# Convolved feed-forward: one 512-wide matmul for high weights, VectorE adds the halves, GpSimd takes the scaling, the product and the low parts

## The chip, the cores and the metric

The kernel runs on one core of a Trainium2 chip. The metric is the device time of one execution in microseconds (us), the median over several runs. A core has five engines that run their own instruction streams and meet at semaphores: PE (TensorE, matmuls), DVE (VectorE), ACT (ScalarE), POOL (GpSimd) and SP (here only the issuer of the weight stream's transfers). In the profile PEld is PE's weight load.

## The reference, cut to what matters

The program is a whole first transformer block with four mixers, followed by a second block of two layers. The change touches one stage of the first block, its feed-forward network with a short causal convolution over the sequence. With `x` the normed rows (256 tokens, 1024 wide):

```python
u = x @ w_up                         # 1024 -> 2 * 2816: gate half and value half
u = conv_w[2]*u[t] + conv_w[1]*u[t-1] + conv_w[0]*u[t-2] + conv_b
hidden = silu(gate) * value          # 2816 wide
out = hidden @ w_down                # 2816 -> 1024, then normed and added to h
```

All of it is float32. Matmuls are done in split form: every operand is a high part (rounded to the matmul's float32r) and a low part (what the rounding left), and a product is high*high + high*low + low*high, three matmuls that add into one PSUM sum.

## The kernel before

**The weight stream.** All weights come from one DRAM tensor in slots of 1 MB (128 partitions x 2048 columns). SP loads slot n into a ring of four once slot n-4 is used up. ACT copies a loaded slot to its high part (`split_high`, L436, output `high`), and DVE subtracts to get the low part (`split_low`, L447, `low<-raw,high`), which lies over the raw slot. PE may start on a slot when its low part is there. ACT and DVE keep three slots ahead of the one just used: in step f of the stage below they split the slot of tile f+3.

**The convolved stage (`Ffn` with `conv=True`).** Its up phase runs over 22 tiles f of 128 hidden features. A tile uses one slot: 8 pieces for the gate and 8 for the value (`part` 0 and 1). The weight piece is the stationary operand, and the 256 tokens of `xh` or `xl` are the moving one: `mm3` (L481 to L483) gives three matmuls of 256 columns for each piece, 48 for a tile, into one PSUM bank `f % 4`. From there each tile goes through a chain of small steps, with its buffers in the tile `square`:

- DVE L1335 multiplies the sums by the row of inverse norms (`inv_row`) into `scaled_in`, 512 wide;
- ACT L1299 (twice, 256 wide) applies tap 2 and the bias into `mixed`;
- DVE L1353 (four times) adds taps 1 and 0, both operands in SBUF;
- ACT L1307 applies Silu to the gate;
- DVE L1365 multiplies gate and value into `product`;
- ACT L1311 copies the product's high part into `hh`, and DVE L1369 subtracts the low part into `hl`.

DVE and ACT run a hand-written order: in step f DVE does the scaling of tile f, the taps of tile f-1, product and low part of earlier tiles, then one `split_low`. Engines work their queues strictly in order, so a wait in a row holds all rows behind it.

**The down phase** (`Residual.tensor`) then runs over 22 tiles of `hh` and `hl`, 11 slots in all, with 512-wide matmuls into banks 4 to 7. It takes the next stage's slots from the same ring, and 24 dummy matmuls (L494) stand at its end. GpSimd in this stage only starts transfers (`Loads`): two that spread bias rows in DRAM, then one of bias into SBUF (L580). All engines meet at the end of a stage (L2720), GpSimd with its transfers landed.

Of the kernel before, what the change touches and what calls it, by code (L numbers as in the profile page):

```python
# [31 lines left out]
P = 128  # L32
S = 256
# [265 lines left out]
def pack_band_bias(x):  # L299
# [15 lines left out]
         "keys_scored", "keys_positive", "keys_summed", "lam_sums", "lam_exps", "masks_added"]  # L315
# [14 lines left out]
class Core:  # L330


    def __init__(self, nc, stream):
# [14 lines left out]
        self.xh = t("xh", [P, KT, S], F32R)  # L348
        self.xl = t("xl", [P, KT, S], F32R)
# [717 lines left out]
class Residual(Stage):  # L1067
# [69 lines left out]
    def row_factor(self, b):  # L1137
        return self.factor
# [100 lines left out]
class Ffn(Residual):  # L1239
# [16 lines left out]

    def row_factor(self, b):
        return self.core.inv[:, 4 + b:5 + b]

    def tensor(self, pe, s):  # L1260
        c = self.core
        self.rows.begin(pe, s)
        for f in range(FT):
            if f == 1:
                self.rows.row(pe, s)
            if f >= 4:
                pe.wait_ge(s["partial_ready" if self.conv else "gates_ready"], f - 3)
            for part in range(2):
                for k in range(KT):
                    if f == 0 and part == 0:  # L1270
# [3 lines left out]
                    last = mm3(pe, c.bank[f % 4][:, part * S:(part + 1) * S], c.piece(pe, self.up, i),  # L1274
                               (c.xh[:, k, :], c.xl[:, k, :]), k == 0, k == KT - 1)
                    c.release(last, self.up, i)
        super().tensor(pe, s)
# [4 lines left out]
    def scalar(self, act, s):  # L1282
# [4 lines left out]
        late = 1 if self.conv else 0  # L1287

        c.split_high(act, self.up.first)
        for step in range(FT + 1 + late):  # L1290
            if step < FT:
                c.split_high(act, self.up.first + step + 1)
            if step < FT and self.conv:
                f = step
# [8 lines left out]
            if 0 <= step - late < FT:  # L1303
                f = step - late
                act.wait_ge(s["convolved"], f + 1)
                gate = self.mixed[:, f % 3, 0:S] if self.conv else self.silu[:, f % 3, :]
                act.activation(gate, gate, ACT.Silu).then_inc(s["inputs_ready"], 1)  # L1307
            if 0 <= step - late - 1 < FT:
                f = step - late - 1
# [4 lines left out]
    def vector(self, dve, s):  # L1314
# [5 lines left out]
        taps, late = 0, 1 if self.conv else 0  # L1320
        row = c.inv_row[:, :]

        c.split_low(dve, self.up.first)
        for step in range(FT + 2 + late):
            if step < FT:
                f = step
# [3 lines left out]
                ps = c.bank[f % 4]  # L1330
                if self.conv:
                    if f >= 2:
                        dve.wait_ge(s["scores_ready"], f - 1)
                        dve.wait_ge(s["convolved"], f - 1)
# [1451 lines left out]
```

## Time and profile before

| what | us |
|---|---|
| median of 3 runs | 1660.08 |
| lowest and highest of them | 1658.35, 1664.02 |
| the profiled execution's own time | 1660.82 |
| its span, first to last instruction | 1659.0 |
| convolved stage, up phase: first matmul to first one of the down phase | 299.16 to 428.22 |
| its down phase, to the dummy matmuls | 428.22 to 488.09 |

Times in rows are us from the span's start. A matmul's own duration in a row is its latency; how fast matmuls follow each other is read from their starts or from their count in a window. A row with xN merges N instructions. Text in brackets at the end of a row is idle time of that engine before it, and what ended it.

### The profile page before, as it was taken

To read this page: it belongs to the slowest core of one execution; us is meant where nothing else is said; L and a number is where in the kernel's file an instruction comes from. 1 tells how busy PE (TensorE), PEld (TensorE's weight loads), DVE (VectorE), ACT (ScalarE), POOL (GpSimd) and SP (SyncE) were. 2 spreads that over 40 slices of the span, in tenths; PEclk is the share of its full clock that TensorE was granted. 3 is DMA by queue.
4 is the path that set the end of the run, shared out by engine and by line. 5 is a ranking of instruction groups with operands and counts; after the bars stand their busy time and mean duration, and the time that the engine had idled before them with its cause. 6 is when DMAs were issued, how large, how long until landed. Compare 5 with 4: busy or idle time off the path is not lost.

```text
span 1659.0 us, 21003 instructions
## 1 busy us (share of the span) xinstructions
PE 1612.4 (97%) x8524; PEld 1364.0 (82%) x8524; DVE 1018.5 (61%) x1379; ACT 863.3 (52%) x1193; POOL 33.7 (2%) x35
## 2 busy tenths in 40 slices
PE   9989999999999999999899999999999999999998
PEld 8878877999888888877777888888888888778887
DVE  5565578698755554568866555455544775765543
ACT  5365675566545443555666444354434565654441
POOL 0000002000000000002000000000000000000000
PEclk9999999999999999999999999999999999999999
DMA  7742324765544555544243655555554533435543
GB/s 286 289 167 108 127 104 176 286 225 189 183 178 178 180 185 193 178 152 153 71 159 130 222 181 180 201 177 178 188 192 178 178 127 127 152 128 190 191 178 127
DMA packets 42959, 289.95 MB, mean 175 GB/s; under 512 B 5048, under 2 KB 5198, under 8 KB 9968
## 3 DMA queue, kind: packets, MB, share of 16 engines
q1 hardware_dynamic: 38272, 271.93, 45.5%
q0 software_dynamic: 4592, 16.69, 2.9%
q8 instruction: 68, 1.11, 0.3%
q14 instruction: 27, 0.22, 0.0%
HBM read 287.51 MB, written 8.55 MB: 178 GB/s over the span
## 4 chain that ended last, share of the span: by engine, by line
PE 87%; DVE 6%; ACT 3%; DMA 2%; issue 1%; DVEq 0%; PEldq 0%; SPq 0%; ACTq 0%; POOL 0%; PEld 0%
PE bank L481 26%; PE bank L483 26%; PE bank L482 25%; PE bank L487 5%; DVE low L447 2%; DMA raw<-stream_dram 2%; PE bank L763 1%; ACT high L436 1%; PE bank L1401 1%; PE bank L645 1%; DMA h<-x_dram 0%; PE bank L1989 0%; PE bank L1843 0%; DVE h L1182 0%; DVE prob L1796 0%
## 5 line engine op out<-in xcount | busy, mean ns | idle before, releaser
L447 DVE TENSOR_TENSOR low<-raw,high 128x2048 fp32r<-128x2048 f32 x254 | 581.2, 2297 | 376.6 <-ACT high L436 376.0
L436 ACT ACTIVATE high<-raw 128x2048 fp32r<-128x2048 f32 x256 | 486.9, 1913 | 350.3 <-DMA raw<-stream_dram 345.6
L481 PE MATMUL bank<-high,xh 128*128 128x512 f32 (+1 forms) x1232 | 486.1, 395 | 6.5 <-DVEq L2720 3.5
L483 PE MATMUL bank<-high,xl 128*128 128x512 f32 (+1 forms) x1232 | 477.8, 388 | 0.0
L482 PE MATMUL bank<-low,xh 128*128 128x512 f32 (+1 forms) x1232 | 477.1, 387 | 0.0
L481 PEld LDWEIGHTS bank<-high,xh 128*128 128x128 f32 x1232 | 232.1, 188 | 54.7 <-DVE low L447 4.6
L483 PEld LDWEIGHTS bank<-high,xl 128*128 128x128 f32 x1232 | 231.9, 188 | 48.4
L482 PEld LDWEIGHTS bank<-low,xh 128*128 128x128 f32 x1232 | 232.3, 189 | 44.5
L481 PE MATMUL bank<-high,hh 128*128 128x512 f32 x440 | 171.9, 391 | 0.0
L483 PE MATMUL bank<-high,hl 128*128 128x512 f32 x440 | 171.3, 389 | 0.0
L482 PE MATMUL bank<-low,hh 128*128 128x512 f32 x440 | 171.2, 389 | 0.0
L481 PE MATMUL bank<-xh,high 128*128 128x256 f32 x472 | 134.3, 285 | 1.2 <-DVE low L447 1.2
L482 PE MATMUL bank<-xl,high 128*128 128x256 f32 x472 | 133.6, 283 | 0.0
L483 PE MATMUL bank<-xh,low 128*128 128x256 f32 x472 | 133.5, 283 | 0.0
L1452 ACT ACTIVATE square<-bank,inv 128x256 f32<-128x256 f32 x88 | 41.7, 475 | 150.0 <-PE bank L483 150.0
L483 PEld LDWEIGHTS bank<-high,hl 128*128 128x128 f32 x440 | 82.6, 188 | 17.3
L482 PEld LDWEIGHTS bank<-low,hh 128*128 128x128 f32 x440 | 82.6, 188 | 16.9
L481 PEld LDWEIGHTS bank<-high,hh 128*128 128x128 f32 x440 | 82.6, 188 | 16.9
L481 PEld LDWEIGHTS bank<-xh,high 128*128 128x128 f32 x472 | 90.6, 192 | 2.2 <-issue 2.2
L482 PEld LDWEIGHTS bank<-xl,high 128*128 128x128 f32 x472 | 90.6, 192 | 0.0
L483 PEld LDWEIGHTS bank<-xh,low 128*128 128x128 f32 x472 | 90.6, 192 | 0.0
L1475 DVE TENSOR_TENSOR square<-square,bank 128x256 f32<-128x256 f32 x88 | 37.1, 422 | 72.7 <-ACT square L1452 72.7
(242 smaller groups left out, 1522.2 us busy)
## 6 DMA issues: line engine op xcount, KB each, us to landing
raw<-stream_dram SPq DMA_DIRECT2D x257, 1024.0 KB, 4.8
band_wide_dram<-band_rows_dram POOLq DMA_DIRECT2D x1, 3072.0 KB, 33.4
t_wide_dram<-t_rows_dram POOLq DMA_DIRECT2D x1, 2304.0 KB, 17.1
u<-mem_dram POOLq DMA_DIRECT2D x2, 1024.0 KB, 5.1
bias<-band_wide_dram POOLq DMA_DIRECT2D x1, 2048.0 KB, 14.3
rel_wide_dram<-rel_rows_dram POOLq DMA_DIRECT2D x1, 1920.0 KB, 17.1
bias<-t_wide_dram POOLq DMA_DIRECT2D x1, 1536.0 KB, 10.7
bias<-rel_wide_dram POOLq DMA_DIRECT2D x1, 1280.0 KB, 7.0
```

The source lines that it names most:

```text
L436: act.activation(self.high[:, n % RING, :], self.raw[:, n % RING, :], ACT.Copy).then_inc(self.high_split, 1)
L447: dve.tensor_tensor(self.low[:, n % RING, :], self.raw[:, n % RING, :], self.high[:, n % RING, :].bitcast(F32), ALU.subtract).then_inc(sel ...
L481: pe.matmul(out, lh, rh, start=start, stop=False)
L482: pe.matmul(out, lh, rl, start=False, stop=False)
L483: return pe.matmul(out, ll, rh, start=False, stop=stop)
L487: return pe.matmul(out, left, right, start=start, stop=stop)
L645: last = pe.transpose(self.bank(g)[0:width, j * P:(j + 1) * P], src, self.core.ident)
L763: last = pe.transpose(self.bank(k)[:, at:at + P], self.rows[:, b, from_tile:from_tile + P], self.core.ident)
L1401: last = pe.transpose(self.turned(c)[:, at:at + P], self.product_rows[:, c % 2, b, j * P:(j + 1) * P], self.core.ident)
L1452: act.activation(self.gate_rows[:, c % 2, b, :], self.sums(c, b)[:, 0:S], ACT.Silu, scale=core.inv[:, 2 + b:3 + b]).then_inc(s["inputs_rea ...
L1475: dve.tensor_tensor(self.product_rows[:, c % 2, b, :], self.gate_rows[:, c % 2, b, :], self.sums(c, b)[:, S:HALF], ALU.mult).then_inc(s["g ...
```

## The change

- `xh` and `xl` become the two halves of one tile `xhl`, so that one access reads 256 columns of high rows and 256 of low rows as a 512-wide moving operand.
- `mm_both` takes the place of `mm3` in the up phase: one 512-wide matmul with the high weights (sums of high rows in the bank's left half, of low rows in its right half), and one 256-wide matmul with the low weights into the left half. Each part of a tile now takes a bank of its own, eight in all.
- ACT copies the right halves to SBUF (`c.t`, twice 256 wide), and DVE adds left half and copy into `scaled_in` (twice 256 wide, `halves_added`).
- GpSimd runs a loop of its own: it scales `scaled_in` by the row (512 wide), makes the product and the low part. It starts its transfers behind this loop, where they stood at the stage's start.
- Silu comes one step later, the copy of the high part too. The other two classes of the stage keep their code.

```diff
+def mm_both(pe, out, weights, rows, start, stop):
+    high, low = weights
+    pe.matmul(out, high, rows, start=start, stop=False)
+    return pe.matmul(out[:, 0:S], low, rows[:, 0, :], start=False, stop=stop)
...
+    def gpsimd(self, pool, s):
...
+        for step in range(FT + 4 if self.conv else 0):
+            f = step
+            if f < FT:
+                pool.wait_ge(s["halves_added"], 2 * f + 2)
...
+                pool.tensor_tensor(scaled, scaled, row, ALU.mult).then_inc(s["partial_ready"], 1)
+            f = step - 4
+            if f >= 0:
+                pool.wait_ge(s["highs_ready"], f + 1)
+                pool.tensor_tensor(c.hl[:, f, :], self.product[:, f % 2, :], c.hh[:, f, :].bitcast(F32), ALU.subtract)\
+                    .then_inc(s["hidden_ready"], 1)
+            f = step - 2
+            if 0 <= f < FT:
+                pool.wait_ge(s["inputs_ready"], f + 1)
+                if f >= 2:
+                    pool.wait_ge(s["hidden_ready"], f - 1)
+                pool.tensor_tensor(self.product[:, f % 2, :], self.mixed[:, f % 3, 0:S], self.mixed[:, f % 3, S:HALF],
+                                   ALU.mult).then_inc(s["gates_ready"], 1)
+        Residual.gpsimd(self, pool, s)
...
-                    last = mm3(pe, c.bank[f % 4][:, part * S:(part + 1) * S], c.piece(pe, self.up, i),
-                               (c.xh[:, k, :], c.xl[:, k, :]), k == 0, k == KT - 1)
+                    last = mm_both(pe, self.sums(f, part), c.piece(pe, self.up, i), c.xhl[:, :, k, :],
+                                   k == 0, k == KT - 1)
...
+                act.wait_ge(c.slot_used, self.up.first + f + 1)
...
+                    last = act.activation(c.t[:, 2 * (f % 2) + part, :], self.sums(f, part)[:, S:HALF], ACT.Copy)
+                last.then_inc(s["side_copied"], 1)
+                c.split_high(act, self.up.first + f + 1)
...
+                dve.wait_ge(s["side_copied"], f + 1)
+                for part in range(2):
+                    dve.tensor_tensor(self.scaled_in[:, f % 2, part * S:(part + 1) * S], self.sums(f, part)[:, 0:S],
+                                      c.t[:, 2 * (f % 2) + part, :], ALU.add).then_inc(s["halves_added"], 1)
```

On DVE, in the middle of the up phase, one step before (L1335 scaling, L1353 taps, L1365 product, L1369 low part, L447 weight split):

```order
L1335 TENSOR_TENSOR square<-bank,inv_row 128x512 [waits convolved_even,scores_ready_even,slot_used]
L1353 SCALAR_TENSOR_TENSOR square<-square,param 128x255 [waits scores_ready_even]
L1353 SCALAR_TENSOR_TENSOR square<-square,param 128x255
L1353 SCALAR_TENSOR_TENSOR square<-square,param 128x254 [waits dve_step_even] x2
L1365 TENSOR_TENSOR square<-square 128x256 [waits hidden_ready_even,inputs_ready_even]
L1369 TENSOR_TENSOR hl<-square,hh 128x256 [waits highs_ready_even]
L447 TENSOR_TENSOR low<-raw,high 128x2048 [waits high_split]
```

The same step on DVE after the change (L1375 adds, L1387 taps):

```order
L1375 TENSOR_TENSOR square<-bank,t 128x256 [waits convolved_even,side_copied_even,scores_ready_even,slot_used]
L1375 TENSOR_TENSOR square<-bank,t 128x256
L1387 SCALAR_TENSOR_TENSOR square<-square,param 128x255 [waits scores_ready_even]
L1387 SCALAR_TENSOR_TENSOR square<-square,param 128x255
L1387 SCALAR_TENSOR_TENSOR square<-square,param 128x254 [waits dve_step_even] x2
L447 TENSOR_TENSOR low<-raw,high 128x2048 [waits high_split]
```

Product and low part have left DVE's step, and its first row now waits for ACT's copy as well (`side_copied`).

On POOL after the change, the last full step of the up phase and the end of its loop (L1277 scaling, L1281 low part, L1288 product, L589 transfers); before, the three transfers were all that it had in this stage:

```order
L1277 TENSOR_TENSOR square<-square,inv_row 128x512 [waits halves_added_even]
L1281 TENSOR_TENSOR hl<-square,hh 128x256 [waits highs_ready_even]
L1288 TENSOR_TENSOR square<-square 128x256 [waits hidden_ready_even,inputs_ready_even]
L1281 TENSOR_TENSOR hl<-square,hh 128x256 [waits highs_ready_even]
L1288 TENSOR_TENSOR square<-square 128x256 [waits hidden_ready_even,inputs_ready_even]
L1281 TENSOR_TENSOR hl<-square,hh 128x256 [waits highs_ready_even]
L1288 TENSOR_TENSOR square<-square 128x256 [waits hidden_ready_even,inputs_ready_even]
L1281 TENSOR_TENSOR hl<-square,hh 128x256 [waits highs_ready_even] x2
L589 DMA t_wide_dram<-t_rows_dram 1536x1x384
L589 DMA band_wide_dram<-band_rows_dram 2048x1x384
L589 DMA bias<-t_wide_dram 128x12x256 [waits loaded]
```

The first three rows are one step, of three operations, each with all operands in SBUF; the transfers stand behind the last low part.

On ACT after the change, the last of the 22 steps (L1332 copies, L436 weight split, L1339 Silu, L1346 tap 2 and bias, L1353 high part) and the end of the loop:

```order
L1332 ACTIVATE t<-bank 128x256 [waits halves_added_even,slot_used]
L1332 ACTIVATE t<-bank 128x256
L436 ACTIVATE high<-raw 128x2048 [waits slot_loaded1]
L1339 ACTIVATE square<-square 128x256 [waits convolved_even]
L1346 ACTIVATE square<-square,param 128x256 [waits gates_ready_even,partial_ready_even]
L1346 ACTIVATE square<-square,param 128x256
L1353 ACTIVATE hh<-square 128x256 [waits gates_ready_even]
L1339 ACTIVATE square<-square 128x256 [waits convolved_even]
L1353 ACTIVATE hh<-square 128x256 [waits gates_ready_even]
L1339 ACTIVATE square<-square 128x256 [waits convolved_even]
L1353 ACTIVATE hh<-square 128x256 [waits gates_ready_even] x2
L436 ACTIVATE high<-raw 128x2048 [waits slot_loaded2]
```

The copies stand ahead of the weight split, and the split of the down phase's fourth slot stands behind the last tile's whole chain.

## Rows read from the trace of the kernel before

**Rows 1.** The page: busy us, share of span and instructions of each engine.

```profile
PE 1612.4 (97%) x8524; PEld 1364.0 (82%) x8524; DVE 1018.5 (61%) x1379; ACT 863.3 (52%) x1193; POOL 33.7 (2%) x35
```

**Rows 2.** Busy time by windows: up phase's middle, down phase's middle, granted clock behind.

```profile
core 0: us, PE busy (x) PEld busy (x) DVE busy (x) ACT busy (x) POOL busy (x), PEclk, DMA share, GB/s
...
430.00:485.00 55.00, 55.00 (x244) 45.53 (x244) 29.51 (x29) 23.17 (x23) 0.00 (x0) 1.00 0.54 191
360.00:400.00 40.00, 40.00 (x335) 40.00 (x335) 35.65 (x56) 25.24 (x36) 0.00 (x0) 1.00 0.52 185
```

**Rows 3.** Timeline of PE: start us, us, engine, line, operation, count.

```profile
428.22 0.40 PE L481 MATMUL bank<-high,hh 128*128 128x512 f32 x1
...
488.09 3.03 PE L494 MATMUL bank<-xh 128*128 128x256 f32 x24
```

**Rows 4.** Timeline of DVE: one step of the up phase, to the next's start.

```profile
334.01 0.69 DVE L1335 TENSOR_TENSOR square<-bank,inv_row 128x512 f32<-128x512 f32 x1
334.61 1.66 DVE L1353 SCALAR_TENSOR_TENSOR square<-square,param 128x255 f32<-128x255 f32 x4
336.18 0.42 DVE L1365 TENSOR_TENSOR square<-square 128x256 f32<-128x256 f32 x1
336.52 0.42 DVE L1369 TENSOR_TENSOR hl<-square,hh 128x256 fp32r<-128x256 f32 x1
336.85 2.29 DVE L447 TENSOR_TENSOR low<-raw,high 128x2048 fp32r<-128x2048 f32 x1
339.06 0.69 DVE L1335 TENSOR_TENSOR square<-bank,inv_row 128x512 f32<-128x512 f32 x1
```

**Rows 5.** Timeline of ACT: reads of a bank, then two rows of a step.

```profile
297.92 3.72 ACT L772 ACTIVATE xh<-bank,param 128x256 fp32r<-128x256 f32 x8 [2.50 <-PE bank L763]
...
346.33 1.08 ACT L1299 ACTIVATE square<-square,param 128x256 f32<-128x256 f32 x2
347.31 0.40 ACT L1307 ACTIVATE square<-square 128x256 f32<-128x256 f32 x1
```

**Rows 6.** Timeline of POOL and DVE in the merge stage, where both work.

```profile
249.84 2.56 POOL L1652 TENSOR_TENSOR xn<-xn,u 128x512 f32<-128x512 f32 x2 [189.33 <-DVE u L1621]
249.75 2.05 DVE L1621 TENSOR_TENSOR u<-u,bank 128x512 f32<-128x512 f32 x3
...
252.35 3.34 POOL L1652 TENSOR_TENSOR xn<-xn,u 128x512 f32<-128x512 f32 x1
254.47 3.38 DVE L447 TENSOR_TENSOR low<-raw,high 128x2048 fp32r<-128x2048 f32 x1
255.65 3.34 POOL L1652 TENSOR_TENSOR xn<-xn,u 128x512 f32<-128x512 f32 x1
```

**Rows 7.** POOL and DVE in a later stage; last, DVE L2101 (min/median/max ns).

```profile
779.68 0.72 POOL L1686 TENSOR_TENSOR u<-bias,taken 128x256 f32<-128x256 f32 x1 [96.83 <-ACTq L2720]
788.23 1.27 POOL L1686 TENSOR_TENSOR u<-bias,taken 128x512 f32<-128x512 f32 x1
788.85 0.67 DVE L2101 TENSOR_TENSOR rden<-rden,small 128x2 f32<-128x2 f32 x1
L2101 DVE TENSOR_TENSOR rden<-rden,small x16: 160/161/665, 142.8 to 799.5; 128x2 f32<-128x2 f32 x16
```

**Rows 8.** The stage's transfers, the late slot; PE's waits (total us, times, longest).

```profile
298.32 1.13 POOL L580 DMA_DIRECT2D t_wide_dram<-t_rows_dram  x1 [39.33 <-DVEq L2720]
333.12 1.05 POOL L580 DMA_DIRECT2D bias<-t_wide_dram  x1 [32.60 <-DMA band_wide_dram<-band_rows_dram]
bias<-t_wide_dram POOLq DMA_DIRECT2D x1, 1536.0 KB, 10.7
320.09 1.91 ACT L436 ACTIVATE high<-raw 128x2048 fp32r<-128x2048 f32 x1 [9.62 <-DMA raw<-stream_dram]
PE bank L481 <- DVE low L447: 1.6, 2, 1.2
```

**Rows 9.** Timeline of DVE: the first tile's scaling.

```profile
308.65 0.69 DVE L1335 TENSOR_TENSOR square<-bank,inv_row 128x512 f32<-128x512 f32 x1
```

**Rows 10.** Busy time by windows: attention, where PE has gaps (columns: PE, PEclk, DMA).

```profile
800.00:812.00 12.00, 10.02 (x78) 1.00 0.00 0
```

More of the change, by code:

```diff
@@ L347, in __init__ @@
         self.h = t("h", [P, NB, D])
[L348 to L349 removed]
+        self.xhl = t("xhl", [P, 2, KT, S], F32R)
+        self.xh, self.xl = self.xhl[:, 0, :, :], self.xhl[:, 1, :, :]
         arena = self.top
@@ L1255, in __init__, with sums @@
         self.scaled_in = part(2 * S + 3 * HALF, 2, HALF)
+    def sums(self, f, part):
+        return self.core.bank[2 * (f % 4) + part][:, :]
+    def gpsimd(self, pool, s):
+        c = self.core
+        row = c.inv_row[:, :].unsqueeze(1).to_broadcast([P, 2, S])
+        for step in range(FT + 4 if self.conv else 0):
+            f = step
+            if f < FT:
+                pool.wait_ge(s["halves_added"], 2 * f + 2)
+                scaled = self.scaled_in[:, f % 2, :].rearrange("p (a t) -> p a t", a=2)
+                pool.tensor_tensor(scaled, scaled, row, ALU.mult).then_inc(s["partial_ready"], 1)
[12 more added lines that the diff above has]
+        Residual.gpsimd(self, pool, s)
     def row_factor(self, b):
@@ L1286, in scalar @@
         bias = PARAM(c.param, "conv_b")
-        late = 1 if self.conv else 0
         c.split_high(act, self.up.first)
[L1290 to L1294, printed above, removed]
+        for step in range(FT + 3):
+            f = step
+            if f < FT:
+                act.wait_ge(c.slot_used, self.up.first + f + 1)
+                if f >= 2:
+                    act.wait_ge(s["halves_added"], 2 * f - 2)
+                for part in range(2):
+                    last = act.activation(c.t[:, 2 * (f % 2) + part, :], self.sums(f, part)[:, S:HALF], ACT.Copy)
+                last.then_inc(s["side_copied"], 1)
+                c.split_high(act, self.up.first + f + 1)
+            f = step - 2
+            if 0 <= f < FT:
+                act.wait_ge(s["convolved"], f + 1)
+                gate = self.mixed[:, f % 3, 0:S]
+                act.activation(gate, gate, ACT.Silu).then_inc(s["inputs_ready"], 1)
+            f = step
+            if f < FT:
                 act.wait_ge(s["partial_ready"], f + 1)
@@ L1302, in scalar @@
                 last.then_inc(s["scores_ready"], 1)
[L1303 to L1309, printed above, removed]
+            f = step - 3
+            if 0 <= f < FT:
                 act.wait_ge(s["gates_ready"], f + 1)
@@ L1319, in vector @@
         w = PARAM(c.param, "conv_w").rearrange("p (j f) -> p j f", j=3)
-        taps, late = 0, 1 if self.conv else 0
-        row = c.inv_row[:, :]
         c.split_low(dve, self.up.first)
-        for step in range(FT + 2 + late):
-            if step < FT:
-                f = step
+        for step in range(FT + 1):
+            f = step
+            if f < FT:
                 dve.wait_ge(c.slot_used, self.up.first + f + 1)
```

39 lines of the change are left out of this document (9 added, 30 removed).

## Prediction

> **What bounds the kernel now.** I read the page's first part, then busy time by windows around the changed stage, then the timelines of DVE and ACT inside it, and last every place where POOL computes. On the page PE is busy for 97% of the span and POOL for 2% [rows 1]. In the middle of the up phase PE starts 335 matmuls in 40 us, 119.4 ns each at full granted clock, while DVE is busy for 35.65 of the 40 [rows 2]: PE sets the pace, DVE comes next. A tile costs PE 48 x 119.4 ns = 5.73 us. One step of DVE from one scaling to the next takes 339.06 - 334.01 = 5.05 us [rows 4], with no gap in it, so DVE has 0.68 us to spare per tile. This spare time is all that the stage has on that engine.
>
> **PE's part.** In the down phase 244 matmuls, 512 wide, start in 55 us, 225.4 ns each [rows 2]. So a 512-wide and a 256-wide one cost 344.8 ns where three 256-wide ones cost 358.2 [rows 2]: no column is saved, only 13.4 ns of fixed cost per piece. A tile falls from 5.73 to 16 x 344.8 ns = 5.52 us, and 22 tiles save 22 x 0.21 = 4.7 us, 0.3% of the kernel. The Trainium skill ("TensorE: Matmul & The Clock Gate", Back-to-back issue gap) gives a warm start-to-start time of N/2.4 ns plus about 2.5 ns, by which one start fewer per piece would save some 0.9 us in all, an estimate; the rows here show more per start, and I go by the rows.
>
> **DVE's part, alone.** From the step's starts in [rows 4]: the 512-wide scaling 0.60, the taps 1.57, product 0.34, low part 0.33, weight split 2.21. Scaling, product and low part leave (1.27). Two 256-wide adds come; as one 256-wide row holds the queue 0.34, they cost 0.68. DVE alone would need 5.05 - 1.27 + 0.68 = 4.46 us per tile.
>
> **POOL's part, alone.** Nearest rows: 0.72 us for a 256-wide operation on two SBUF operands, 1.27 for a 512-wide one [rows 7]. A step's three operations take 1.27 + 2 x 0.72 = 2.71. Taken engine by engine all is below PE's 5.52, and the change would win its 4.7. That is the reading that I don't follow, for the next reason.
>
> **What the two do to each other.** In the merge stage POOL's 512-wide operations take 1.28 us beside DVE rows with one operand in a bank, and those DVE rows keep their 0.68 (three in 2.05) [rows 6]. But beside the weight split, whose operands are both in SBUF, each waits for the whole of the other: POOL 3.34, the split 3.38 instead of 2.29, POOL 3.34 [rows 6]. The ends are 255.69 (POOL), 257.85 (DVE) and 258.99 (POOL): 2.16 for the split, 1.14 for the POOL operation, one after the other, 3.30 a pair. A DVE operation of 2 columns with both operands in SBUF takes 0.67 instead of 0.16 and ends with the POOL operation that it met [rows 7]. In the changed stage four taps and the split of every DVE step have both operands in SBUF, and so have all three POOL operations; only the adds (one operand in a bank) are free of it. No row shows a tap (scalar_tensor_tensor) beside POOL; I take it to behave like the split, since what they share is two SBUF operands.
>
> The Trainium skill ("SBUF — State Buffer", Who interferes with whom) says that any DVE instruction with two SBUF inputs contends with a GpSimd instruction that reads SBUF, and that the later one waits for all of the earlier one. The trace agrees where it can show it (3.34 and 3.38 above); for the taps no row does. By that rule the sum below stands; without it for the taps, the first rival does.
>
> **The step after.** A 256-wide POOL operation holds DVE for its 0.72 less the 0.14 that the 512-wide one loses (1.28 to 1.14): 0.58. So DVE's step is adds 0.68 + taps 1.57 + split and POOL's scaling 3.30 + two more holds 1.16 = 6.71 us, longer than PE's 5.52. Why all of POOL's work falls there: the scaling of tile f is released by DVE's own adds, and DVE goes straight on to taps; product and low part follow on POOL at once, as Silu of that tile was done during the step before. ACT stays hidden: copies 0.93 (2 of 3.72/8, [rows 5]), split 1.91 [rows 8], Silu 0.40, taps' first part 0.98 (to the next start), high copy as long as Silu, 0.40 [rows 5], together 4.6. From below the step is 6.71 - 0.68 = 6.03, if POOL gets a full 0.68 beside the adds; from above 4.46 + 2.71 = 7.17, with POOL's whole durations. I take 6.71, from the rows of just this pair.
>
> **The sum.** DVE's first add stands where the first scaling did, 308.65 [rows 9]. Behind the adds (0.68) the weight split starts at once and holds up POOL's scaling: 308.65 + 0.68 + 2.16 = 311.5. Then scaling 1.14, ACT's two rows 0.98, its copies of the next tile 0.93, three hand-overs of 0.1 (my estimate): step 1 begins at 314.8. Step 1 has the scaling alone on POOL, 0.68 + 1.57 + 3.30 = 5.55, to 320.4; steps 2 and 3 a product more, 6.13 each, to 332.6; steps 4 to 21 are full, 18 x 6.71 = 120.8, to 453.4. PE waits from about tile 7 on, some 1.2 us per tile, since each step's split frees a tile three further on. The last three splits are those of the down phase's first three slots, the third at 453.4, and PE works on it until 453.4 + 5.44 = 458.8 (59.87 us for 11 slots, [rows 3]). The fourth slot's high copy stands on ACT behind the last tile's whole chain: taps with two POOL holds 2.73, Silu 0.40, product 0.72, high copy 0.40, ACT's split 1.91, DVE's 2.29, six hand-overs 0.6, together 9.05, to 462.5. Eight slots remain, 43.5 us: the down phase ends at 506.0, where it ended at 488.09 [rows 3]. That is 17.9 us later: 1660.8 + 17.9 = 1678.7 by the profiled execution, and as this lies 0.7 above the median of the runs, **1678**. The part before the stage and the stages behind it keep their code; I cost them at nothing.
>
> **The moved transfers.** Before, they start at 298.32 and hold the weight stream up: ACT waits 9.62 us for one slot and PE at most 1.2 us [rows 8]. That wait goes, but gives nothing, as DVE's chain is then what PE waits for. They now start behind POOL's last low part, at about 459. The two spreads take 333.12 - 298.32 = 34.8 us and the bias 1.05 + 10.7 [rows 8], to about 506; PE ends its dummy matmuls 3 us after 506.0. So they are just covered. Bounds: nothing, or up to 2 us of slot waits on PE (the 1.2 scaled to two late slots) and up to 6 us if they last 10 us longer and the stage's end waits for POOL. I take nothing, the burst meeting a ring that filled while PE waited.
>
> **Rivals.**
> - *The taps don't exclude POOL.* Then only the split waits, for at most product and low part: 4.46 + 1.16 = 5.62 a step. 314.8 + 21 x 5.62 = 432.8, the chain of the last tile without its two holds 7.9, to 440.7, eight slots, 484.2: 3.9 us earlier, **1656** for the median, not slower. For it: no row shows a tap beside POOL. Against it: the three kinds of DVE row that are shown differ in just the operands' place. Chance 0.10.
> - *PE keeps the pace throughout*, since POOL slips in between: -4.7 and the 1.2 of the late slot, **1654**. It needs DVE's step below 5.52, and the holds alone bring it to 6.03 at the least. 0.04.
> - *More is lost:* POOL's full durations (18 x 0.46 = 8.3 more) or transfers that outlast the stage (6 more): **1686 to 1693**. For it: three hand-overs a tile between POOL and others, for which no row has a price. 0.06 beyond the forecast's own range.
> - *The clock falls*, as PE now has a gap in each tile: a tile of 11 us, **1700 and far more**. Against it: PE was busy for 10.02 of 12 us in attention and kept the granted clock of 1.00 [rows 10], and 5.52 of 6.71 is about the same share. 0.02.
>
> **How the numbers follow.** The forecast has 0.78. Its own range goes by the step's bounds: 18 x 0.68 = 12.2 less is 1666, 18 x 0.46 = 8.3 more is 1686. About 0.3%, 5 us, is what a measurement of this kernel can tell from no change. The range from 1661 to 1691 holds the forecast and most of the third rival and leaves out the first two and the fourth. Faster by over 0.3%: 0.04 (the second rival). Within: 0.12 (the first, and 0.02 of the forecast's lower end). Slower: 0.84.
>
> **What would show it.** In the profile after: DVE's four taps with POOL between them, about 3.9 us from the first tap to the split where it was 1.57; starts of the adds 6.7 us apart; PE waiting for `low` about 1.2 us at nearly each tile from the seventh on and some 3.6 us ahead of the down phase's fourth slot; matmuls of a tile at 5.5 us when they run. The forecast is wrong if the taps keep 0.39 us each beside POOL rows, or if POOL's rows fall mainly beside the adds.

## Result, and the profile after

The changed kernel takes 1681.03 us (median of 4 runs, 1679.15 to 1683.04), the kernel before, run beside it, 1662.05 us (4 runs, 1658.35 to 1664.21). The ratio is 1.0112 with an interval of 1.0092 to 1.0132: slower by 19.0 us, where the prediction said 1678, 17.9 us more than before. The profiled execution took 1680.24 us, its span is 1678.4 us, 19.4 us longer than before at the same granted clock (0.995 and 0.996).

The page's first line now, to be read beside [rows 1]:

```profile
PE 1615.1 (96%) x8172; PEld 1346.4 (80%) x8172; DVE 1045.0 (62%) x1357; ACT 872.4 (52%) x1237; POOL 105.3 (6%) x101
```

PE starts 352 matmuls fewer. DVE has 22 instructions fewer and 26.5 us more busy time. That is the whole case in one row: work was taken off DVE, and DVE became longer. The timeline of DVE shows one step in the middle of the up phase, to the next step's adds (compare [rows 4]):

```profile
383.50 0.74 DVE L1375 TENSOR_TENSOR square<-bank,t 128x256 f32<-128x256 f32 x2
384.17 3.68 DVE L1387 SCALAR_TENSOR_TENSOR square<-square,param 128x255 f32<-128x255 f32 x4
387.77 2.28 DVE L447 TENSOR_TENSOR low<-raw,high 128x2048 fp32r<-128x2048 f32 x1
389.98 0.74 DVE L1375 TENSOR_TENSOR square<-bank,t 128x256 f32<-128x256 f32 x2
```

From start to start the adds take 0.67 us, the four taps 3.60 (1.57 before), the split 2.21; the step is 6.48 us here and 6.49 as the mean of the 18 full steps (331.80 to 448.65).

The timeline of POOL in the same step has its three rows beside the taps:

```profile
384.32 1.48 POOL L1277 TENSOR_TENSOR square<-square,inv_row 128x512 f32<-128x512 f32 x1 [3.23 <-DVE square L1375]
385.76 0.92 POOL L1281 TENSOR_TENSOR hl<-square,hh 128x256 fp32r<-128x256 f32 x1
386.82 0.75 POOL L1288 TENSOR_TENSOR square<-square 128x256 f32<-128x256 f32 x1
```

The first steps, in which POOL's rows arrive one by one, give the price of each. In this timeline of DVE, step 1 has only POOL's scaling, step 2 the product as well:

```profile
315.03 2.70 DVE L1387 SCALAR_TENSOR_TENSOR square<-square,param 128x255 f32<-128x255 f32 x4
317.65 2.28 DVE L447 TENSOR_TENSOR low<-raw,high 128x2048 fp32r<-128x2048 f32 x1
...
320.51 3.19 DVE L1387 SCALAR_TENSOR_TENSOR square<-square,param 128x255 f32<-128x255 f32 x4
323.62 2.28 DVE L447 TENSOR_TENSOR low<-raw,high 128x2048 fp32r<-128x2048 f32 x1
```

The taps take 2.62 us, then 3.11, then 3.60 in the full steps, after 1.57 before: POOL's 512-wide row holds DVE (DVE stands still for it) for 1.05 us, each 256-wide one for 0.49. These are the rows' own durations, 1.28 and 0.72 [rows 6, 7], less 0.23 each time.

PE's waits for `low` in the up phase (us in all, times, longest), where before there were two of 1.6 us together [rows 8]:

```profile
PE bank L495 <- DVE low L447: 8.3, 14, 0.7
```

Five more, 7.9 us in all, stand in the down phase, and one of 3.08 ahead of the next stage. The timeline of PE has the fourth down slot, a later slot, the dummy matmuls and the next stage's start (`DVEq L2741` is DVE's arrival at the meeting that ends the stage):

```profile
457.27 0.47 PE L481 MATMUL bank<-high,hh 128*128 128x512 f32 x1 [2.70 <-DVE low L447]
...
481.71 0.47 PE L481 MATMUL bank<-high,hh 128*128 128x512 f32 x1 [2.43 <-DVE low L447]
...
503.59 3.03 PE L503 MATMUL bank<-xhl 128*128 128x256 f32 x24
...
509.70 1.07 PE L772 MATMUL bank<-const,h 128*128 128x128 f32 x8 [3.08 <-DVEq L2741]
```

The wait at 457.27 is the last tile's chain. The waits at 481.71 and 509.70 come from weight slots that land late, as two rows of ACT show:

```profile
477.32 1.92 ACT L436 ACTIVATE high<-raw 128x2048 fp32r<-128x2048 f32 x1 [15.08 <-DMA raw<-stream_dram]
...
502.31 1.92 ACT L436 ACTIVATE high<-raw 128x2048 fp32r<-128x2048 f32 x1 [2.67 <-DMA raw<-stream_dram]
```

The moved transfers run from 453.87 to about 502.4 us, and a weight slot takes longer to land while they do. Time from issue to landing of the slots issued from 457 to 505 us, after the change and, for comparison, in the run below that spreads the transfers out:

```profile
DMA to landing us min/median/max: 4.8/9.8/14.3
```

```profile
DMA to landing us min/median/max: 4.7/4.8/4.9
```

The 14.3 belong to the slot that ACT splits at 477.32; it was issued at 463.0.

The down phase ends 15.50 us later than before (503.59 against 488.09), the next stage begins 18.05 later (509.70 against 491.65), and within that stage another 1.36 us go, between two groups of its transposes (511.19 to 514.22, before 493.14 to 494.81). PE does not wait there; its granted clock is at the lower of its two levels, 1.2 GHz instead of 2.4. Busy time by windows of that place after the change, and of the same place before (PE busy, matmuls begun, granted clock, DMA share, GB/s):

```profile
511.00:514.00 3.00, 2.81 (x8) 0.50 0.00 0
```

```profile
493.00:496.00 3.00, 2.86 (x15) 1.00 0.38 158
```

From there to the end the two traces keep their distance of 19.4.

### The profile page after: what moved, and what is told of

The parts are those of the page before. It is cut to its first block, busy times and chain, and to the rows that moved or that the text cites. A ratio compares the mean times of both kernels' runs of the same rounds, so it can differ in the third digit from the quotient of the medians.

```text
span 1678.4 us, 20429 instructions
## 1 busy us (share of the span) xinstructions
PE 1615.1 (96%) x8172; PEld 1346.4 (80%) x8172; DVE 1045.0 (62%) x1357; ACT 872.4 (52%) x1237; POOL 105.3 (6%) x101
## 4 chain that ended last, share of the span: by engine, by line
PE 78%; DVE 11%; issue 4%; ACT 3%; DMA 3%; POOL 1%; DVEq 0%; SPq 0%; ACTq 0%; PEldq 0%; PEld 0%
PE bank L481 23%; PE bank L483 23%; PE bank L482 23%; PE bank L487 5%; DVE square L1387 4%; DVE low L447 2%; DMA raw<-stream_dram 2%; PE bank L772 2%; ACT high L436 1%; PE bank L1422 1%; DVE square L1375 1%; PE bank L654 1%; POOL square L1277 0%; DMA h<-x_dram 0%; PE bank L2010 0%
## 5 line engine op out<-in xcount | busy, mean ns | idle before, releaser
L447 DVE TENSOR_TENSOR low<-raw,high 128x2048 fp32r<-128x2048 f32 x254 | 580.9, 2296 | 373.8 <-ACT high L436 373.2
L436 ACT ACTIVATE high<-raw 128x2048 fp32r<-128x2048 f32 x256 | 486.6, 1913 | 320.7 <-DMA raw<-stream_dram 314.1
L481 PE MATMUL bank<-high,xhl 128*128 128x512 f32 (+1 forms) x1232 | 487.2, 395 | 6.9 <-DVEq L2741 4.8
L483 PE MATMUL bank<-high,xhl 128*128 128x512 f32 (+1 forms) x1232 | 478.8, 389 | 0.0
L482 PE MATMUL bank<-low,xhl 128*128 128x512 f32 (+1 forms) x1232 | 477.9, 388 | 0.0
L481 PEld LDWEIGHTS bank<-high,xhl 128*128 128x128 f32 x1232 | 233.0, 189 | 55.0 <-DVE low L447 6.0
L483 PEld LDWEIGHTS bank<-high,xhl 128*128 128x128 f32 x1232 | 232.4, 189 | 48.5
L482 PEld LDWEIGHTS bank<-low,xhl 128*128 128x128 f32 x1232 | 233.1, 189 | 44.6
L495 PE MATMUL bank<-xhl,high 128*128 128x512 f32 x352 | 125.4, 399 | 8.3 <-DVE low L447 8.3
L481 PEld LDWEIGHTS bank<-high,hh 128*128 128x128 f32 x440 | 82.6, 188 | 26.5 <-issue 9.7
L496 PE MATMUL bank<-xhl,low 128*128 128x256 f32 x352 | 98.5, 280 | 0.0
L495 PEld LDWEIGHTS bank<-xhl,high 128*128 128x128 f32 x352 | 66.0, 187 | 26.9 <-issue 12.3
L1387 DVE SCALAR_TENSOR_TENSOR square<-square,param 128x255 f32<-128x255 f32 (+1 forms) x88 | 77.7, 941 | 0.0
L781 ACT ACTIVATE xhl<-bank,param 128x256 fp32r<-128x256 f32 x96 | 38.1, 478 | 55.3 <-PE bank L772 55.0
L496 PEld LDWEIGHTS bank<-xhl,low 128*128 128x128 f32 x352 | 66.4, 189 | 0.0
```

Source lines behind the costliest of these rows:

```text
L436: act.activation(self.high[:, n % RING, :], self.raw[:, n % RING, :], ACT.Copy).then_inc(self.high_split, 1)
L447: dve.tensor_tensor(self.low[:, n % RING, :], self.raw[:, n % RING, :], self.high[:, n % RING, :].bitcast(F32), ALU.subtract).then_inc(sel ...
L481: pe.matmul(out, lh, rh, start=start, stop=False)
L482: pe.matmul(out, lh, rl, start=False, stop=False)
L483: return pe.matmul(out, ll, rh, start=False, stop=stop)
L495: pe.matmul(out, high, rows, start=start, stop=False)
```

## Experiments

Two theories stood against each other. **Holds:** two operands in SBUF are what DVE and POOL cannot have at once, so POOL's rows lengthen DVE's step. **Hand-overs:** the chain through POOL, with its semaphores, sets the step, whatever the operands. Beside them the moved transfers were open: the prediction took them at nothing. "Stage" below is the time from PE's first transposes of the convolved stage to those of the next: 194.17 us before, 212.38 after. "Up phase" is counted from the same transposes to the down phase's first matmul, some 1.7 us more than in the table of the time before: 130.74 us before, 138.10 after.

### All vector work back on DVE

```diff
...
-        for step in range(FT + 4 if self.conv else 0):
...
+                dve.wait_ge(s["halves_added"], 2 * f + 2)
...
+                dve.tensor_tensor(scaled, scaled, row, ALU.mult).then_inc(s["partial_ready"], 1)
...
+                dve.tensor_tensor(c.hl[:, f, :], self.product[:, f % 2, :], c.hh[:, f, :].bitcast(F32), ALU.subtract)\
...
+                dve.tensor_tensor(self.product[:, f % 2, :], self.mixed[:, f % 3, 0:S], self.mixed[:, f % 3, S:HALF],
+                                  ALU.mult).then_inc(s["gates_ready"], 1)
```

> The changed kernel with the two-matmul form kept, but scaling, product and low part back on DVE; GpSimd only starts its transfers, at the stage's start as in the kernel before. Exclusion theory (DVE and POOL wait for each other when both read two operands in SBUF): no POOL work, so no holds. DVE's step is adds 0.66 + scaling about 0.57 + taps 1.57 + product 0.34 + low part 0.33 + weight split 2.20 = 5.67 us, the taps at 0.39 each; the stage is back within 3 us of before, 1658 to 1665 us, although DVE has 1.2 us more work per tile than in the changed kernel. Rival (the two-matmul form, the ACT copies or the longer chain of hand-overs cost the time, not POOL): the step stays near 6.4 us and the time at 1675 us or above.

Measured: 1671.35 us (8 runs, 1667.41 to 1674.08), ratio 1.0042 (1.0026 to 1.0058). Timeline of DVE:

```profile
384.29 0.75 DVE L1357 TENSOR_TENSOR square<-bank,t 128x256 f32<-128x256 f32 x2
385.07 0.69 DVE L1361 TENSOR_TENSOR square<-square,inv_row 128x512 f32<-128x512 f32 x1
385.69 1.66 DVE L1372 SCALAR_TENSOR_TENSOR square<-square,param 128x255 f32<-128x255 f32 x4
387.26 0.42 DVE L1380 TENSOR_TENSOR hl<-square,hh 128x256 fp32r<-128x256 f32 x1
387.78 0.42 DVE L1387 TENSOR_TENSOR square<-square 128x256 f32<-128x256 f32 x1
388.12 2.29 DVE L447 TENSOR_TENSOR low<-raw,high 128x2048 fp32r<-128x2048 f32 x1
390.33 0.75 DVE L1357 TENSOR_TENSOR square<-bank,t 128x256 f32<-128x256 f32 x2
```

With more work of its own, and POOL idle, DVE's step is 6.04 us instead of 6.48, and the kernel is 9.7 us faster than the changed one. The taps are back at 1.57 from start to start. My time was too low: I had added up the rows to 5.67. The rest are two places where DVE waits for its own last row: adds to scaling 0.78 where the adds need 0.67, low part to product 0.52 where one such row needs 0.34; and the scaling, with both operands in SBUF, takes 0.62. So the step stays above PE's tile (5.65 us by the dearer of two prices, below), the stage takes 204.10 us, and the kernel stays above the one before.

### Memory fills on POOL

POOL writes constants for about as long, and nothing reads two SBUF operands there. This run leaves out the scaling, the product and the low part.

```diff
-                pool.tensor_tensor(scaled, scaled, row, ALU.mult).then_inc(s["partial_ready"], 1)
...
+                pool.memset(c.t[:, 4:9, :], 0.0).then_inc(s["partial_ready"], 1)
...
-                pool.tensor_tensor(self.product[:, f % 2, :], self.mixed[:, f % 3, 0:S], self.mixed[:, f % 3, S:HALF],
-                                   ALU.mult).then_inc(s["gates_ready"], 1)
...
+                pool.memset(c.t[:, 13:15, :], 0.0)
+                pool.memset(self.product[:, f % 2, :], 0.5).then_inc(s["gates_ready"], 1)
```

> The changed kernel with POOL's three operations per tile replaced by fills (memset) of similar length that read nothing from SBUF: 1280 columns in place of the scaling, 512 + 256 in place of product and of low part. The sums stay unscaled, and hidden and its low part are constants, so the stage's result is not computed; every wait and signal between the engines is kept. Exclusion theory: POOL stays busy for some 2.5 to 3 us per tile and the chain of hand-overs is as long, but the taps are back at 0.39 us each (1.57 for four instead of 3.60) and DVE's step is PE's, 5.5 us; the adds start about 5.5 us apart and the up phase ends near 422. Rival (the hand-overs through POOL set the step): adds stay about 6.4 us apart.

Measured: 1667.05 us (one run). The stage takes 193.67 us. Timeline of DVE:

```profile
383.49 0.76 DVE L1377 TENSOR_TENSOR square<-bank,t 128x256 f32<-128x256 f32 x2 [1.12 <-ACT t L1334]
384.16 1.66 DVE L1389 SCALAR_TENSOR_TENSOR square<-square,param 128x255 f32<-128x255 f32 x4
385.74 2.29 DVE L447 TENSOR_TENSOR low<-raw,high 128x2048 fp32r<-128x2048 f32 x1
389.14 0.76 DVE L1377 TENSOR_TENSOR square<-bank,t 128x256 f32<-128x256 f32 x2 [1.11 <-ACT t L1334]
```

All hand-overs through POOL are still there, and POOL is busy for 18.76 of 40 us, but the taps keep 1.57 and DVE sits idle 1.1 us per step: PE sets the pace, with a tile of 5.65 us where I had given 5.5. The hand-overs alone don't make the step.

### The kernel before, with late transfers

```diff
+    def gpsimd(self, pool, s):
+        if self.conv:
+            pool.wait_ge(s["hidden_ready"], FT)
+        Residual.gpsimd(self, pool, s)
```

> The kernel before with one thing moved: GpSimd starts the stage's transfers only behind the last low part of the up phase (about 437), not at the stage's start. Theory of the moved transfers: the wait of 1.2 us at the stage's start goes; in the down phase one slot comes late (PE waits about 2.4 us), at the stage's end another holds DVE's last rows up (about 2.5 us), and the next stage loses about 1.3: 4 to 5.5 us slower than before, about 1666. Rival (the transfers are covered, as the prediction had them): 0 to 1.2 us faster than before.

Measured: 1665.5 us (12 runs), ratio 1.0014 (0.9997 to 1.0031). The early stall of 1.2 us [rows 8] is gone, but the stage ends with a wait of 2.23 us, and it is 1.3 us longer; as the early stall went, the late transfers cost it 2.5 us. This is between the theories: in the kernel before, whose PE sets the pace, late transfers cost less than I expected, and the ratio can't be told from none.

### The changed kernel, with the transfers spread out

```diff
+            if step in (4, 10):
+                dst, src = self.loads.ahead.pairs[0 if step == 4 else 1]
+                pool.dma_start(dst, src).then_inc(c.loaded, 16)
+                c.loads += 1
+            if step == 16:
+                self.loads.ahead.finish(c, pool)
+                Loads(*self.loads.pairs).start(c, pool)
...
```

> The changed kernel with GpSimd's transfers spread over the up phase: one spread at step 4, the other at step 10, the bias at step 16 of POOL's loop. Theory of the moved transfers: the late slots of the down phase and of the stage's end go (2.4 + 2.5 + 1.3 us of the 19.4), at the price of about 1.1 us of POOL's queue for each start, part of it on DVE's step: 1674 to 1677 us. Rival (they cost nothing, the 19 us are all DVE's step and the tail): 1680 to 1684.

Measured: 1677.77 us (4 runs), ratio 1.0082 (1.0059 to 1.0106). PE at the start of the next stage:

```profile
509.22 1.06 PE L772 MATMUL bank<-const,h 128*128 128x128 f32 x8 [0.53 <-DVEq L2751]
```

The end's wait is 0.53 instead of 3.08 us, the wait of 2.43 has no counterpart, and the stage takes 208.72 us instead of 212.38. These 3.7 us are fewer than I had given: in this trace the granted clock is 0.72 from 460 to 466 us, behind a wait of 2.65, where eight 512-wide matmuls start up to 0.43 apart instead of 0.23, which costs some 1.6 us; after the change the clock is 1.00 in that place, behind a wait of 2.70. Without it, by this estimate, the place of three transfers is worth 5.3 us in the stage. DVE's step is unchanged (386.69 to 393.16, 6.47 us). The stage behind it takes 190.45 us to a memory fill of POOL that stands alike in all traces, against 191.80 after the change: the low clock at that stage's start is gone too.

### Taps with one operand in the bank

ACT writes its tap-2 result into the right half of the tile's bank, which is free by then, and the taps read it there. Work and chain are otherwise nearly those of the changed kernel: ACT has two more one-column rows per tile, the taps change their order, the first two of them write to the bank as well, and PE waits for the taps (`convolved`) instead of the adds before it uses a bank again.

```diff
-                    last = act.activation(self.mixed[:, f % 3, part * S:(part + 1) * S],
-                                          self.scaled_in[:, f % 2, part * S:(part + 1) * S], ACT.Identity,
-                                          bias=bias[:, col:col + 1], scale=w[:, 2, col:col + 1])
+                    for n, out in ((1, self.mixed[:, f % 3, part * S:part * S + 1]), (S, self.sums(f, part)[:, S:HALF])):
+                        last = act.activation(out, self.scaled_in[:, f % 2, part * S:part * S + n], ACT.Identity,
+                                              bias=bias[:, col:col + 1], scale=w[:, 2, col:col + 1])
...
-                        buf = self.mixed[:, f % 3, at + back:at + S]
...
+                        buf = self.sums(f, part)[:, S + back:HALF]
+                        out = self.mixed[:, f % 3, at + 1:at + S] if j else buf
...
```

> The changed kernel, but ACT writes its tap-2 result into the right half of the tile's bank, and each of DVE's four taps has one operand there (ACT makes one more column, twice per tile, 0.2 us). POOL keeps scaling, product and low part. If two SBUF operands are what holds DVE: taps keep about 0.39 us each beside POOL (1.6 for four, now 3.60), only the weight split can still meet POOL's product or low part (0.49 each), DVE's step is 0.66 + 1.57 + 2.20 + 0.5 to 1.0 = 4.9 to 5.4 us, below PE's 5.65; PE sets the pace, the up phase is 125 to 126 us instead of 138.1, the stage (transfers late as after the change) 194 to 198 instead of 212.4, the time 1661 to 1667, some 16 us below the changed kernel. If instead any work of POOL holds DVE, or the hand-overs through POOL set the step, taps stay at 0.8 us or more, the step at 6.3 or more, the time above 1674.

Measured: 1662.42 us (10 runs, 1659.10 to 1667.50), ratio 1.0002 (0.9990 to 1.0014). Timeline of DVE:

```profile
378.35 0.76 DVE L1375 TENSOR_TENSOR square<-bank,t 128x256 f32<-128x256 f32 x2 [0.56 <-ACT t L1332]
379.02 0.87 DVE L1388 SCALAR_TENSOR_TENSOR bank<-square,param,bank 128x254 f32<-128x254 f32 x2
379.80 0.86 DVE L1388 SCALAR_TENSOR_TENSOR square<-square,param,bank 128x255 f32<-128x255 f32 x2
380.58 2.76 DVE L447 TENSOR_TENSOR low<-raw,high 128x2048 fp32r<-128x2048 f32 x1
383.90 0.76 DVE L1375 TENSOR_TENSOR square<-bank,t 128x256 f32<-128x256 f32 x2 [0.55 <-ACT t L1332]
```

And POOL:

```profile
379.19 1.31 POOL L1277 TENSOR_TENSOR square<-square,inv_row 128x512 f32<-128x512 f32 x1 [0.79 <-DVE square L1375]
380.46 0.74 POOL L1281 TENSOR_TENSOR hl<-square,hh 128x256 fp32r<-128x256 f32 x1
381.34 2.61 POOL L1288 TENSOR_TENSOR square<-square 128x256 f32<-128x256 f32 x1
```

The same POOL rows run beside the same taps. The taps now take 1.56 us (379.02 to 380.58) instead of 3.60, and POOL's scaling 1.31 instead of 1.48. The second pair still writes to SBUF and is not held either, so what counts is the operand that is read. What still meets is the one DVE row with two SBUF operands: the split takes 2.76 instead of 2.28, because POOL's low part was running (0.48), and the product waits for the split (2.61). DVE again waits for ACT and PE, 0.55 us per step. The up phase is 124.8 us, where the kernel before with late transfers has 129.36. That is the whole gain of the 512-wide matmuls, 4.6 us. The down phase gives it back: a slot behind the late transfers costs PE 2.4 us, the granted clock is 0.79 as a mean from 456 to 464 us (at its lower level for part of it), and the stage's end waits for 2.27. The stage is 194.30 us, and the time that of the kernel before.

### Taps in the bank, transfers spread out

Both edits together.

```diff
...
+            if step in (4, 10):
...
+                        buf = self.sums(f, part)[:, S + back:HALF]
...
```

> The kernel with taps in the bank, and the three transfers spread over POOL's steps 4, 10 and 16. If late transfers cost about 5 us: stage 190 to 193 us, next stage 1.3 shorter than behind late transfers, time 1657 to 1660, a ratio to the kernel before of 0.996 to 0.999. If late transfers cost nothing where PE sets the pace: the same time as the run with the taps in the bank and late transfers.

Measured: 1658.61 us (12 runs), ratio 0.9974 (0.9960 to 0.9988), faster than the kernel before. The stage takes 188.23 us against 194.17, less than I had given, as the tile is 5.55 us and not 5.65 (below). Against the run with late transfers this is 6.1 us, with the low clock of that run in it.

### The low part computed twice

```diff
+                pool.wait_ge(s["hidden_ready"], f)
+                pool.tensor_tensor(c.t[:, 4, :], self.product[:, f % 2, :], c.hh[:, f, :].bitcast(F32), ALU.subtract)
```

> The changed kernel with POOL's low part computed twice (a second 256-wide row of 0.74 us per tile into a scratch tile). If POOL's rows hold DVE: one hold more of 0.49 us, DVE's step 6.46 + 0.49 = 6.95, 18 full steps give 9 us, the time about 1690. If the step comes from the hand-overs between engines, not from the holds: POOL has 3.2 us idle in each step and takes the row there, step 6.46, the time 1681 to 1682.

Measured: 1691.28 us (one run). Timeline of DVE:

```profile
383.14 0.74 DVE L1377 TENSOR_TENSOR square<-bank,t 128x256 f32<-128x256 f32 x2
383.80 3.66 DVE L1389 SCALAR_TENSOR_TENSOR square<-square,param 128x255 f32<-128x255 f32 x4
387.38 2.83 DVE L447 TENSOR_TENSOR low<-raw,high 128x2048 fp32r<-128x2048 f32 x1
390.14 0.74 DVE L1377 TENSOR_TENSOR square<-bank,t 128x256 f32<-128x256 f32 x2
```

One more POOL row of 256 columns, whose result nobody uses, makes DVE's step 7.00 us. The taps are as before, and it is now the split that is held, 2.83 instead of 2.28. POOL was idle for 2.9 us in each step; its free time is no room.

### Product and low part on POOL in the kernel before

The kernel before with its three 256-wide matmuls; scaling stays on DVE, the transfers are spread out.

```diff
+    def gpsimd(self, pool, s):
...
+                pool.tensor_tensor(c.hl[:, f, :], self.product[:, f % 2, :], c.hh[:, f, :].bitcast(F32), ALU.subtract)\
...
+                pool.tensor_tensor(self.product[:, f % 2, :], self.mixed[:, f % 3, 0:S], self.mixed[:, f % 3, S:HALF],
+                                   ALU.mult).then_inc(s["gates_ready"], 1)
...
```

> The kernel before, three 256-wide matmuls per piece, with product and low part on POOL instead of DVE and the three transfers spread over POOL's steps 4, 10 and 16; scaling stays on DVE with an operand in the bank. If a POOL row of 0.72 us holds DVE by 0.49: DVE's step is 5.05 - 0.67 + 0.98 = 5.36 us, still below PE's 5.73, so PE sets the pace, tiles stay 5.75 us apart, the up phase is 129.1 to 130.7 us, and the time is that of the kernel before, 2 us less at most. If any POOL work in the step costs its whole length or a hand-over sets the pace: the step passes 5.73 and the time rises by 3 us or more.

Measured: 1658.78 us (10 runs), ratio 0.9986 (0.9971 to 1.0001). Timeline of DVE, then of POOL:

```profile
378.44 0.69 DVE L1362 TENSOR_TENSOR square<-bank,inv_row 128x512 f32<-128x512 f32 x1
379.04 2.14 DVE L1380 SCALAR_TENSOR_TENSOR square<-square,param 128x255 f32<-128x255 f32 x4
381.11 2.28 DVE L447 TENSOR_TENSOR low<-raw,high 128x2048 fp32r<-128x2048 f32 x1
383.31 0.68 DVE L1362 TENSOR_TENSOR square<-bank,inv_row 128x512 f32<-128x512 f32 x1
```

```profile
382.02 1.97 POOL L1270 TENSOR_TENSOR hl<-square,hh 128x256 fp32r<-128x256 f32 x1 [1.91 <-ACT hh L1338]
383.95 1.02 POOL L1277 TENSOR_TENSOR square<-square 128x256 f32<-128x256 f32 x1
```

The step is 4.87 us, not 5.36: only one of the two POOL rows meets a DVE row that it can hold (taps 2.07, 0.50 more). The other waits out the split (1.97) and then runs beside the scaling, which has an operand in a bank and keeps its 0.60. Taking 0.67 off DVE won 0.18, and it is not needed there; the stage is 192.78 us, about the early stall shorter. Here a hold costs nothing, since PE's tile of 5.76 us is above the step. The stage with taps in the bank and spread transfers, 188.23, is 4.6 us shorter than this one; the times of the two kernels, 1658.61 and 1658.78, do not show it.

### All 512-wide matmuls of a part first

The kernel with taps in the bank and spread transfers, but in each part after the first the eight 512-wide matmuls come first, then the eight 256-wide ones.

```diff
...
+                    if k < KT:
+                        pe.matmul(self.sums(f, part), high, c.xhl[:, :, k, :], start=k == 0, stop=False)
+                    else:
+                        last = pe.matmul(self.sums(f, part)[:, 0:S], low, c.xh[:, k - KT, :], start=False, stop=k == 2 * KT - 1)
...
```

> The kernel with taps in the bank and spread transfers; in every part of a tile after the first, PE does the eight 512-wide matmuls with the high weights first, then the eight 256-wide ones with the low weights, 16 starts as before. If the change of width between neighbours makes a pair cost 353 ns where the down phase's and the old up phase's rows give 225 + 119 = 345: tile 5.52 us, up phase some 2.8 us shorter than with alternating widths. If the 512-wide operand of two segments costs it, or the order doesn't matter: tile 5.65, same time as with alternating widths.

Measured: 1656.56 us (5 runs), ratio 0.9964 (0.9952 to 0.9975). Neither theory came out, as both took the alternating order to have one price. Timeline of PE, then:

```profile
335.33 2.00 PE L1318 MATMUL bank<-xhl,high 128*128 128x512 f32 x8
...
357.68 2.00 PE L1318 MATMUL bank<-xhl,high 128*128 128x512 f32 x8
```

Eight parts lie between these two rows: 22.35 us, 2.794 each, a tile of 5.59. With alternating widths a tile has two prices, and they can be read from the starts of two high matmuls, eleven pairs apart, in two kernels, the one with taps in the bank:

```profile
383.95 0.39 PE L495 MATMUL bank<-xhl,high 128*128 128x512 f32 x1
...
387.76 0.39 PE L495 MATMUL bank<-xhl,high 128*128 128x512 f32 x1
```

and the one with memory fills:

```profile
383.91 0.40 PE L495 MATMUL bank<-xhl,high 128*128 128x512 f32 x1
...
387.80 0.40 PE L495 MATMUL bank<-xhl,high 128*128 128x512 f32 x1
```

Eleven pairs take 3.81 us in the one and 3.89 in the other, 346 and 354 ns a pair, and 347 and 353 over longer stretches. The lower is the sum of what rows of one width take: 120.0 ns for a 256-wide matmul (48 in a tile of 5.76 us, kernel before) and 226.7 for a 512-wide one (three in 0.68 us, down phase). In every trace with alternating widths the pair keeps one of these two prices from one wait of PE to the next, and may change at a wait; the changed kernel starts with 347 and has both later. Over the 352 pairs of the up phase 6 to 7 ns are 2.1 to 2.5 us: 124.8 us with taps in the bank against 127.0 with memory fills. What chooses between them is open. The grouped order lies between the two, so it is no step forward from the cheaper one: its stage takes 189.41 us against 188.23. That its median is 2 us below the alternating order's can't be told from the spread of runs (1652.85 to 1663.88 there).

## Why the prediction came out right, and where its terms were off

**DVE's step: mechanism right, size over-stated.** The step was put at 6.71 us from the holds of POOL's rows, and is 6.49. The failing term is what a row loses of its duration when it holds another: I took 0.14 from the one pair in [rows 6] (holds of 1.14, 0.58, 0.58), and the trace shows 0.23 (1.05, 0.49, 0.49). Adds 0.66, taps 1.57, split 2.20 and holds 2.03 make 6.46. The sum priced the scaling by the pair that it makes with the split; it meets the taps, as my signs had it, where the taps took 3.6 us to the split instead of the 3.9 that I gave. At the end of the 18 full steps the prediction was 4.8 us too late (453.4 against 448.65): 4.0 by these steps, 0.35 by the three before them, and 0.45 by the start of the first. PE waits in 14 tiles, as forecast, but 0.6 us in each and not 1.2; the shorter step explains 0.2 of the difference and pairs at the dearer price 0.1, the rest is not worked out.

**The taps' place among the excluded: right.** No row of before showed it. The rule that the prediction took from the Trainium skill ("SBUF — State Buffer", Who interferes with whom) holds here for the taps (scalar_tensor_tensor) too. The four taps take 3.60 us with both operands in SBUF and 1.56 with one in a bank beside the same POOL rows, and the memory fills, which read nothing, hold nobody. In one point the trace differs: the later row loses not the whole of the earlier one but 0.23 us less. The first rival, 1656, is out.

**The tail: right.** Last full step to the fourth down slot was worked out as 9.05 us and is 8.62 (448.65 to 457.27).

**The moved transfers: the step that failed.** They were taken at nothing and cost 5.3 us in the stage. They start at 453.87 and last until about 502.4, near my 459 and 506, and they are just over when PE reaches its dummy matmuls, as I said. But they don't act by lasting too long: they push weight slots aside, which take up to 14.3 us to land instead of 4.8. One lands so late that ACT waits 15.08 us for it and PE 2.43, so that the eight last slots take 46.3 us instead of 43.5. Another holds DVE's last split up to 504.26, and behind it the norm that ends the stage: 6.11 us from the dummies to the next stage where there were 3.56. Before, one slot came 9.62 us late and cost PE 1.2 [rows 8]. I named these prices as bounds and then chose zero, on the ground that the ring would have filled. It had filled: behind the last tile's chain ACT splits three slots, from 452.89 on, without waiting for one. But each further slot is issued only when PE has used one up, and the transfers run for 48 us (453.87 to 502.4). The spread transfers give the same 5.3, an estimate, as 1.6 us of it are the low clock of that run. In the kernel before the late place costs 2.5, so the price depends on the kernel. Another 1.36 us are the low clock in the next stage. One other kernel with late transfers has it (taps in the bank, 0.50 from 492 to 495), three have not (memory fills, late transfers alone, low part twice). It stands behind the longest two of these kernels' waits at the stage's end (3.08 and 2.27 us, the others 2.23, 1.99 and 1.85), and with the transfers spread, where that wait is 0.53, it is gone; so it comes with the late transfers, though not in each kernel. The clock stayed at 1.00 behind a wait of 2.70 in the same kernel, and what brings it down stays open.

**PE's own saving: right where PE sets the pace.** 4.7 us were worked out, and 4.6 are measured with taps in the bank, or 2.3 with memory fills, at the pair's other price, which no row of before showed. In the changed kernel it gives nothing, as predicted, because DVE's step is what PE waits for.

So the mechanism of DVE's step was right, but that the 17.9 us came so near is luck: two errors cancel. Steps and tail were 5.2 us too long (4.8 and 0.4), the transfers 5.3 too short, with the low clock's 1.36 on top: 17.9 - 5.2 + 5.3 + 1.4 is the 19.4 of the spans. The experiments price the two causes apart: the holds, without which the time is that of the kernel before (1662.42), and the transfers, 5.3 us in the stage and 1.4 behind it.

## What to carry to other kernels

Before moving work from VectorE to GpSimd, look at the operands of what remains on VectorE: a row with both operands in SBUF and a GpSimd row with the same hardly overlap, and the idle time of either is no room for the other. One operand in PSUM frees both; here that single edit took the taps from 3.60 to 1.56 us and, with the transfers spread over the stage, turned 1.1% slower into 0.3% faster. And a transfer that is moved should be judged by the weight slots that it delays, not by whether it ends in time.

## What the runs showed of the hardware

- A GpSimd row with two SBUF operands holds a VectorE row with two SBUF operands for its duration less 0.23 us: 1.05 of 1.28 us (512 columns), 0.49 of 0.72 (256 columns). A GpSimd fill holds nobody, and a VectorE row with one operand in a bank is not held.
- Two matmul widths in turn, 512 and 256 columns, have two stable prices a pair, 347 and 353 ns, at the same granted clock of 1.00; rows of one width alone give 226.7 and 120.0, which is 347 together.
- Where VectorE waits for its own last row, it loses 0.1 to 0.18 us (0.78 instead of 0.67, 0.52 instead of 0.34).
- Beside the late transfers a weight slot of 1 MB took 9.8 us to land as a median, up to 14.3, where it takes 4.8 with the transfers spread.
- The granted clock fell to its lower level of 1.2 GHz over 511 to 514 us, behind a wait of PE of 3.08 us, and 512-wide matmuls then started 0.43 us apart instead of 0.23. Behind a wait of 2.70 us, at 457.27 in the same trace, it stayed at the upper one.
